# Passing two tensors of a state-space stage between on-chip buffers in eight small transfers instead of two large ones through device memory

## The reference

```
u = (h @ w_in).reshape(S, G=64, C=16)
bu = einsum('sgc,gpc->sgp', u, bbar)                     # complex, P=64 states a group
x[s] = a * x[s-1] + bu[s]                                # complex, forward in time
y = Re(einsum('sgp,gcp->sgc', x, c)) + d_skip * u
val, gate = split(gelu(y) @ w_glu); out = val * sigmoid(gate)
```

## Time and profile before

| what | value |
|---|---|
| median of 3 runs | 1181.65 us (1181.65 to 1187.68) |
| profiled execution, its own time | 1180.64 us |
| its span, first to last instruction | 1178.6 us |
| PE busy | 1124.9 us, 95% of the span |
| DVE busy | 811.3 us, 69% |
| ACT busy | 456.1 us, 39% |
| mean granted TensorE clock | 0.985 |
| state-space stage, from the first UB to the last `y_lo` | about 628 to 725 us of the span |

### The profile page before, as it was taken

One profiled execution on the slowest core, in us unless ns is written; L12 is line 12 of the kernel. 1 busy time (PEld: TensorE's weight loads), 2 busy tenths in 40 slices (PEclk: granted clock), 3 DMA queues, 4 the chain that ended last, 5 costly groups with the idle time before them and its releaser, 6 DMA issues.

```text
span 1178.6 us, 14622 instructions
## 1 busy us (share of the span) xinstructions
PE 1124.9 (95%) x5596; PEld 912.2 (77%) x5596; DVE 811.3 (69%) x1151; ACT 456.1 (39%) x677; POOL 127.9 (11%) x222
## 2 busy tenths in 40 slices
PE   5899999999999999989999999999999999999995
PEld 4777558788888887868777887887888888888874
DVE  6786655798886888658875884555775367635764
ACT  5422553454522553216452233334443244423441
POOL 3837107900000000000000000000000000000000
PEclk9999999999999999989999989999999999999998
DMA  6222002233333333423345883323232232233221
GB/s 218 74 97 90 1 1 72 72 102 113 104 133 103 126 125 107 126 72 111 108 157 167 238 239 89 112 92 102 90 105 92 94 103 90 90 107 101 87 81 71
DMA packets 61749, 125.60 MB, mean 107 GB/s; under 512 B 21744, under 2 KB 30320, under 8 KB 61680
## 3 DMA queue, kind: packets, MB, share of 16 engines
q1 hardware_dynamic: 60528, 120.48, 32.4%
q0 software_dynamic: 1152, 4.19, 1.1%
HBM read 109.97 MB, written 14.68 MB: 106 GB/s over the span
## 4 chain that ended last, share of the span: by engine, by line
PE 69%; DVE 19%; issue 3%; ACT 3%; DVEq 2%; DMA 2%; SPq 1%; ACTq 0%
PE bank L1168 22%; PE bank L1170 21%; PE bank L1169 21%; DVE WL L659 4%; DVE CV L914 2%; DVE Z L904 1%; DVE MX L777 1%; ACT CV L586 1%; DVE CV L911 1%; PE bank L1383 1%; DVE HH L893 1%; DVE SS L670 1%; DMA ud_scratch<-UB 1%; DVEq L913 1%; DVE Pexp L785 1%
## 5 line engine op out<-in xcount | busy, mean ns | idle before, releaser
L426 ACT ACTIVATE WH<-RAW 128x1024 fp32r<-128x1024 f32 (+1 forms) x184 | 190.0, 1033 | 412.5 <-PE bank L1170 374.5
L1168 PE MATMUL bank<-GH,WH 128*128 128x512 f32 x816 | 323.7, 397 | 19.1 <-DVE GL L697 12.7
L1170 PE MATMUL bank<-GH,WL 128*128 128x512 f32 x816 | 319.1, 391 | 0.0
L1169 PE MATMUL bank<-GL,WH 128*128 128x512 f32 x816 | 319.1, 391 | 0.0
L659 DVE TENSOR_TENSOR WL<-RAW,WH 128x1024 fp32r<-128x1024 f32 (+1 forms) x184 | 221.7, 1205 | 39.9 <-ACT WH L426 39.5
L1168 PE MATMUL bank<-AH,WH 128*128 128x512 f32 x596 | 236.9, 398 | 6.9 <-DVE AL L897 5.8
L1170 PE MATMUL bank<-AH,WL 128*128 128x512 f32 x596 | 233.9, 392 | 0.0
L1169 PE MATMUL bank<-AL,WH 128*128 128x512 f32 x596 | 233.8, 392 | 0.0
L1168 PEld LDWEIGHTS bank<-GH,WH 128*128 128x128 f32 x816 | 154.2, 189 | 54.9 <-issue 13.9
L1169 PEld LDWEIGHTS bank<-GL,WH 128*128 128x128 f32 x816 | 154.2, 189 | 32.6 <-issue 1.2
L1170 PEld LDWEIGHTS bank<-GH,WL 128*128 128x128 f32 x816 | 154.0, 189 | 32.7
(11 more groups left out here) (228 smaller groups left out, 991.2 us busy)
## 6 DMA issues: line engine op xcount, KB each, us to landing
RAW<-in_w_up SPq DMA_DIRECT2D x88, 512.0 KB, 3.5
RAW<-in_w_dn SPq DMA_DIRECT2D x32, 512.0 KB, 3.5
RAW<-in_w_glu SPq DMA_DIRECT2D x16, 512.0 KB, 3.6
RAW<-in_w_dn SPq DMA_DIRECT2D x16, 384.0 KB, 3.0
RAW<-in_w_wo SPq DMA_DIRECT2D x8, 512.0 KB, 3.6
od_scratch<-OO SPq DMA_DIRECT2D x8, 512.0 KB, 3.3
kd_scratch<-KT SPq DMA_DIRECT2D x8, 512.0 KB, 5.0
RAW<-in_w_win SPq DMA_DIRECT2D x8, 512.0 KB, 4.7
```

Of the source, the lines that this page charges most:

```text
L426: act_(WH[b % RH][:, :n], RAW[b % RW][:, :n], ACT.Copy).then_inc(s_hi, 1)
L1168: mm(out, wh, hi_[:, k, :], start=start, stop=False)
L1169: mm(out, wh, lo_[:, k, :], start=False, stop=False)
L1170: return mm(out, wl, hi_[:, k, :], start=False, stop=stop)
```

## The change

Both scratch tensors go away. The layout change is made by eight transfers of 32 KB for each tensor and tile, one for each group g, from 16 partitions of UB to 128 partitions of U2, and back from Y2 to YB. Those of u are issued by SP, now ahead of the round's weight load; of those of y SP issues the four of even groups and ACT, behind `gelu`, the four of odd groups. `gelu` now signals after each of its two halves. The waits follow.

```diff
-            def u_out(j):
+            def u_rows(j):
                 sp.wait_ge(s_ev, FIRST["win"] + j + 1)
-                sp.dma_start(UD[j], UB[j % 2][:]).then_inc(s_uw, 16)
-
-            def u_in(j):
                 if j >= 3:
                     sp.wait_ge(s_Y, j - 2)
-                sp.wait_ge(s_uw, 16 * (j + 1))
-                sp.dma_start(U2[j % 3][:], cmaj(UD[j])).then_inc(s_ur[j % 3], 16)
-
-            def y_out(j):
-                sp.wait_ge(s_g, j + 1)
-                sp.dma_start(cmaj(YD[j]), Y2[j % 2][:]).then_inc(s_yw, 16)
-
-            def y_in(j):
+                for g in range(GJ):
+                    sp.dma_start(U2[j % 3][:, g, :], UB[j % 2][C * g:C * g + C, :, :]).then_inc(s_ur[j % 3], 16)
+
+            def y_rows(j):
                 if j >= 2:
                     sp.wait_ge(s_act, TILE0["y"] + j - 1)
-                sp.wait_ge(s_yw, 16 * (j + 1))
-                sp.dma_start(YB[j % 2][:], YD[j]).then_inc(s_yr[j % 2], 16)
+                sp.wait_ge(s_g, 2 * j + 1)
+                for g in range(0, GJ, 2):
+                    sp.dma_start(YB[j % 2][C * g:C * g + C, :, :], Y2[j % 2][:, g, :]).then_inc(s_yr[j % 2], 16)
 
             def lags_in(j):
+                if j >= 2:
+                    sp.wait_ge(s_Y, j - 1)
@@
             for t in range(NJ + 3):
                 if t < NJ:
+                    u_rows(t)
                     load(FIRST["win"] + 4 + t)
-                    u_out(t)
-                    u_in(t)
                 if t >= 3:
-                    y_out(t - 3)
+                    y_rows(t - 3)
                     if t - 1 < NJ:
                         lags_in(t - 1)
-                    y_in(t - 3)
@@ ScalarE
             def gelu(j):
                 act.wait_ge(s_Y, j + 1)
                 if j >= 2:
-                    act.wait_ge(s_yw, 16 * (j - 1))
+                    act.wait_ge(s_yr[j % 2], 16 * GJ * (j // 2))
                 for gi in range(2):
-                    m = act_(Y2[j % 2][:, gi::2, :], bank[4 + 2 * (j % 2) + gi][:, 0:QJ * NK].rearrange(
-                        "p (a k) -> p a k", k=NK), ACT.Gelu_apprx_tanh)
-                m.then_inc(s_g, 1)
+                    act_(Y2[j % 2][:, gi::2, :], bank[4 + 2 * (j % 2) + gi][:, 0:QJ * NK].rearrange(
+                        "p (a k) -> p a k", k=NK), ACT.Gelu_apprx_tanh).then_inc(s_g, 1)
+
+            def y_rows(j):
+                if j >= 2:
+                    act.wait_ge(s_act, TILE0["y"] + j - 1)
+                act.wait_ge(s_g, 2 * j + 2)
+                for g in range(1, GJ, 2):
+                    act.dma_start(YB[j % 2][C * g:C * g + C, :, :], Y2[j % 2][:, g, :]).then_inc(s_yr[j % 2], 16)
@@
                 if 3 <= t < NJ + 3:
                     gelu(t - 3)
+                    y_rows(t - 3)
@@ VectorE, u_out
                 if j >= 2:
-                    dve.wait_ge(s_uw, 16 * (j - 1))
+                    dve.wait_ge(s_ur[(j - 2) % 3], 16 * GJ * ((j - 2) // 3 + 1))
@@ TensorE, inputs and outputs
-                pe.wait_ge(s_ur[j % 3], 16 * (j // 3 + 1))
+                pe.wait_ge(s_ur[j % 3], 16 * GJ * (j // 3 + 1))
@@
-                    pe.wait_ge(s_g, j - 1)
+                    pe.wait_ge(s_g, 2 * j - 2)
```

More of the change, by code:

```diff
@@ L279, in build @@
         KD_ = nc.dram_tensor("kd_scratch", (NJ, P, LQ, C * LQ), F32, kind="Internal").ap()
-        UD = nc.dram_tensor("ud_scratch", (NJ, P, LQ, NK), F32, kind="Internal").ap()
-        YD = nc.dram_tensor("yd_scratch", (NJ, P, LQ, NK), F32, kind="Internal").ap()
         s_raw = [sem(f"raw{i}_loaded") for i in range(RW)]
@@ L299, in build @@
         s_tmr, s_or = [sem("TM0"), sem("TM1")], [sem("O0"), sem("O1")]
-        s_uw, s_ur = sem("ud_written"), [sem(f"U{i}_loaded") for i in range(3)]
+        s_ur = [sem(f"U{i}_loaded") for i in range(3)]
         s_rt, s_E, s_X, s_Y, s_g = sem("RT"), sem("E"), sem("states"), sem("Y"), sem("gelu")
-        s_yw, s_yr = sem("yd_written"), [sem("YB0_loaded"), sem("YB1_loaded")]
+        s_yr = [sem("YB0_loaded"), sem("YB1_loaded")]
         s_sig = sem("sigmoid")
@@ L314, in span @@
             return range(FIRST[name], FIRST[name] + BLOCKS[name])
-        def cmaj(dram):
-            return bass.AP(dram.tensor, dram.offset, [[NK, P], [C * LQ * NK, GJ], [1, NK]])
         @block.sync
@@ L613, in gelu @@
                 if j >= 2:
-                    act.wait_ge(s_yw, 16 * (j - 1))
+                    act.wait_ge(s_yr[j % 2], 16 * GJ * (j // 2))
                 for gi in range(2):
-                    m = act_(Y2[j % 2][:, gi::2, :], bank[4 + 2 * (j % 2) + gi][:, 0:QJ * NK].rearrange(
-                        "p (a k) -> p a k", k=NK), ACT.Gelu_apprx_tanh)
-                m.then_inc(s_g, 1)
+                    act_(Y2[j % 2][:, gi::2, :], bank[4 + 2 * (j % 2) + gi][:, 0:QJ * NK].rearrange(
[6 more added lines that the diff above has]
+                    act.dma_start(YB[j % 2][C * g:C * g + C, :, :], Y2[j % 2][:, g, :]).then_inc(s_yr[j % 2], 16)
             def y_tile(j):
-                act.wait_ge(s_yr[j % 2], 16 * (j // 2 + 1))
+                act.wait_ge(s_yr[j % 2], 16 * GJ * (j // 2 + 1))
                 act_(AH[:, j, :].rearrange("p (k s) -> p s k", s=LQ), YB[j % 2][:], ACT.Copy).then_inc(s_thi, 1)
```

## The result

The changed kernel takes 1197.97 us in the median of 4 runs (1194.66 to 1202.56), the kernel before 1183.39 us in the runs beside it (1181.65 to 1187.68). The ratio is 1.0106, with a 95% interval of 1.0077 to 1.0135: slower by 1.1%, some 12.5 us by the ratio (the two medians lie 14.6 us apart). 1191.8 us had been forecast, with 1183 to 1199 as range.

A forecast was written before the change was run, and what follows sets the result against it. PE, busy for 95% of the span, was taken to bound the kernel, with only the stage's ends open. 5.3 + 2.5 + 2.4 = +10.2 us on 1180.64 gave 1190.8, plus 1.0 for the median 1191.8 us; range 1183 to 1199.

The forecast's parts named there:

- The price of an issue: SP's queue: each small transfer takes 0.47 us to issue, by the row of the nearest size, 16 KB.
- Start of the stage: Load `win`+5 waits behind u's issues until 637.0, lands at 642.4; PE waits longer for the first states: +5.3 us.
- The clock: Start of the stage: a PE wait of some 6 us brings the lower clock, +2.5 us, ends 0 and 5.2.
- The middle: Middle rounds: loads come 2.7 us late, but DVE's lead of 5.35 us takes it up: zero.
- End of the stage: TM of tile 6 is issued at 695.9 in place of 693.29 and lands later: +2.4 us, low clock unchanged.
- y: y's path loses a hop, but PE has no wait for `y_lo` in this stage: worth nothing.
- SP becomes the bound: Rival, 8%: from 0.8 us an issue SP can't keep up with PE; at 1.02, near 1212 us.
- issues are hidden: Rival, 10%: issues hold SP 0.1 us or less, the end loses its wait and low clock: faster, 1173.5 us.
- prices are small: Rival, 20%: the waits at both ends grow by only 2.7 us, 4.3 with a short clock fall: 1184 to 1187.5.

The follow-up runs named there:

- experiment 4: Changed kernel with u's eight copies moving 16 rows of 2 KB to the same partitions, without the layout change: 1198.55 us, ratio 1.0117 to the kernel before.
- experiment 5: Changed kernel with five extra matmuls on constant data ahead of PE's wait for `states(0)`: 1195.79 us, ratio 1.0098 to the kernel before.
- experiment 3: Changed kernel with only y direct; u goes through device memory as before, load ahead of it: 1185.01 us, ratio 1.0002 to the kernel before.
- 6: Changed kernel with the weight load ahead of u and u's odd groups issued by POOL, not SP: 1187.03 us, ratio 1.0006 to the kernel before.
- 1: Changed kernel with SP's weight load put back ahead of u's eight issues: 1192.61 us, ratio 1.0069 to the kernel before.
- y off SP: Kernel before with y direct, even groups issued by POOL and odd by ACT; u through device memory: 1184.34 us, ratio 0.9994 to the kernel before.
- u alone: Changed kernel with only u direct; y goes through device memory in two large transfers as before: 1201.15 us, ratio 1.0136 to the kernel before.
- 11: Kernel before with three extra matmuls on constant data ahead of PE's wait for TM of tile 6: 1182.34 us, ratio 0.9971.

## Why the prediction was right, and where its sizes were off

The forecast direction, place and mechanism held; the time lies 6.2 us above the forecast and 1.0 below the upper end of the range. Of the 6.2 us, 1.7 are the kernel before, whose median beside these runs was 1183.39 and not 1181.65. The sum had 10.2 us; the stage of the profiled execution shows 17.0, and the timed runs 12.5.

- **The price of an issue: 0.47 us taken, 0.64 measured**, with no difference between long and short runs (experiment 4). The row of 16 KB at the kernel's start was the nearest but not the price in this list. The range's ends took it in only in part. The rule of the Trainium skill (DMA: Bandwidth & Descriptors, Issuing engines are not separate DMA queues) compares one initiating with one transfer, and so taken it isn't contradicted here: 0.60 us beside a landing of 3.3 (median). It doesn't carry over to a row of them: eight issues, 5.1 us, took longer than the landing of one, since the issues follow each other and the landings overlap.
- **Start of the stage: +5.3 taken.** The load of `win`+5 went out later than predicted, at 643.91, which is 641.2 when the stage's later start is taken off, in place of 637.0; but it landed in 3.9 us and not in 5.4. `states(0)` came 7.9 us later than before. PE's added waiting is 6.2 us. 2.1 us of it are before `inputs(0)`, which I had left out: I looked at U2(1) and not at U2(0), whose eight issues took 6.4 us. That 6.2 lies near 5.3 is in part luck: the load went out 4.2 us later than forecast and landed 1.5 sooner, and PE, held up and at half clock before, came 3.8 us later to the wait for the states.
- **The clock: +2.5 taken, 5.8 measured at the start and 3.0 at the end**: this term failed most. After the wait of 2.1 us half clock came for 3.4 us, and after the wait of 4.9 us for 10.2: together 1.7 + 4.1 = 5.8 us lost at the start, above the end of 5.2 that I had named. At the end, which I had put at "0 within 1.7", the half clock lasted 20 us in place of 10 and cost 3.0 us more. That it follows a wait, and costs about what was measured, experiment 5 shows at the start.
- **The middle: zero taken, zero waits.** The loads came late in every round (ACT's `hi` now waits for each, where it waited for PE before) and DVE's lead took it up, until `states(5)`: PE's 3.23 us of waiting for them are this lateness, for which the prediction had added nothing.
- **End of the stage: +2.4 taken, +2.0 of waiting measured**, but in other places. TM of tile 6 went out at 713.03, 8.6 us after `outputs(4)` and not 6.1, and yet PE did not wait for it: the wait was 1.67 us for TM of tile 5 and 3.23 for the states, and PE, at half clock, then came late enough for tile 6. The size was right by luck.
- **y: nothing taken, nothing measured** (experiment 3).
- **Rivals.** That SP becomes the bound was put at 0.8 us an issue; at 0.64 its rounds of 9.0 to 10.3 us still fit into PE's 10.65. That issues are hidden is excluded. That prices are small is excluded, too.

The cause of the loss is settled for the start: the order and the number of u's issues on SP, by the timed runs of experiments 3 and 6 and the profiles of 1 and 5. What each part of it costs is read from single profiles. What remains of the wait at the end of the stage, in both kernels, isn't a matter of SP's order alone, since the TM that PE waited for took from 4.2 us (changed kernel) to 9.2 (y off SP) to land; whether a third TM buffer or an earlier O2 would remove it was not tried.

## What to carry to other kernels

Replacing two large hops by eight small transfers moves the cost from the landing, which nobody may be waiting for, to the queue that issues them, where everything behind it waits: count the issues of a round, and ask what stands behind them that an idle engine needs next. Look at the first and the last tile of a pipeline for themselves; the lead that hides a late load in the middle isn't there at either end. And price a wait of PE of some 2 us or more with the half clock that follows it, which in the changed kernel cost as much again as the waits.

## What the runs showed of the hardware that wasn't expected

- An issue on SP in this list takes 0.60 us (median) plus 0.04 to the next, 0.62 together where the 32 KB are 16 long rows and not 128 short runs; at the kernel's start it was 0.43. On ACT four took 2.5 to 2.9 us, on POOL eight 4.5. What sets the 0.60 against the 0.43 stays open.
- Half clock behind a wait lasted 3.4 us (behind 2.10 us for U2(0)) to 20.5 us (behind 1.67 for TM and 3.23 for the states) in the changed kernel, and 23.9 us with u alone (6.33 for TM); the stretches of 10 us and more in these two began inside the wait. Waits of 1.19, 1.42 and 1.52 us before `inputs(0)` (experiments 4, 2 and 11) left the clock at 1.00; waits of 1.83 and 1.92 us there (1 and 5) were followed by 3.4 us at 0.50. The Trainium skill (TensorE: Matmul & The Clock Gate, HAM oscillation — how this bites in real kernels) has a wait for a transfer as such a cause; the traces agree, with 3.4 us at 0.50 behind the 2.10 us for U2(0).
- Transfers asked for close together landed later: with y off SP the weight load was asked for 0.6 to 0.9 us behind TM, and its landing (median) went from 4.8 to 9.3 us and TM's from 5.2 to 7.7, with the kernel's time unchanged (ratio 0.9994).
